# A rotary rotation without a permutation matmul: VectorE shuffles partner rows out of the projection's bank

## The chip, the cores and the metric

The kernel runs on one core of one Trainium2 chip. The metric is device time in microseconds of one execution, as the median of several. The engines are TensorE (PE, with its weight loads as PEld), VectorE (DVE), ScalarE (ACT), GpSimd (POOL) and the queue that issues most transfers (SP). Each works through its own list of instructions in order and waits on semaphores for the others.

## The reference

Two transformer blocks over 1024 tokens of width 1024, in float32, one after the other. Only the first half of the first block's attention concerns the change: four "differential" heads, each with two q and two k vectors of 64 rows, of which the first 16 rows are rotated by position.

```python
h = rmsnorm(x, norm1_g[l])
proj = jnp.einsum('bsd,de->bse', h, w_in[l])
dq, dk, dv, fq, fk, fv, fg = jnp.split(proj, SPLITS, axis=-1)
dq = rope_partial(dq.reshape(B, S, DIFF_HEADS, 2, DIFF_DH), cos, sin)
dk = rope_partial(dk.reshape(B, S, DIFF_HEADS, 2, DIFF_DH), cos, sin)
...
def rope_partial(t, cos, sin):            # half = 8
    t1 = t[..., :half]
    t2 = t[..., half:ROPE_DIM]
    return jnp.concatenate([t1 * c - t2 * s, t2 * c + t1 * s, t[..., ROPE_DIM:]], axis=-1)
...
p = softmax(mask(q1 k1)) - lam * softmax(mask(q2 k2));  od = rmsnorm(p v, subln_g) * (1 - lam_init)
```

After these come eight "fox" heads with a decay bias and no rotation, the output projection, a gated feed-forward layer, and the second block.

## The kernel before

Everything lies transposed: 128 rows of features on the partitions, 1024 tokens in two halves of 512 columns along the free side. A float32 product is made of three faster ones: each operand is split into a high and a low part, and for every 128-row step PE issues high by high (L1810), low weights by high (L1812) and high weights by low (L1815), each 128x512. I call these three a group; a projection of 128 features for one half is eight groups into one PSUM bank. The weights come from DRAM in pieces of four steps; ACT rounds a piece to its high part (L2421) and POOL subtracts for the low part (L2670, "lows"). PE has to have both.

The first block's attention runs in units: a0 to a3 (differential, one head each), then b0 to b3 (fox). While unit n goes through scores, softmax and values, the dense groups of unit n+1's q, k and v projection are put between its steps as filler; a0's own projection runs at the start, beside the first norm. For each half of q and of k of units a0 to a3 the steps are:

- DVE evacuates the bank into a stage buffer and multiplies by the norm factor `rstd` (for q also by 0.125): L2080, L2082.
- Three groups later PE multiplies the stage by a permutation matrix in plain float32, which brings each row its partner row eight rows away (L1868), into the next dense bank.
- DVE multiplies that bank by the table of sines into a second stage buffer (L2089), POOL multiplies the first stage by cosines (L2676) and adds both (L2694).
- ACT copies the sum to its high part (L2504, L2505), POOL makes the low parts in two instructions (L2707, L2709), SP moves some of them to other partitions, and the scores may start.

A sub-norm closes each differential unit: ACT squares (L2546), PE sums over partitions (L1936), DVE turns the sum into a mean (L2165), ACT takes Ln and Exp (L2552, L2556, each behind a table load), POOL does five instructions per half (L2716 to L2725).

Buffers: five stage buffers (four more in the start), handed out in turn; whoever takes one waits for the events that gave it back. In units a0 to a3 the dense groups use PSUM banks 6 and 7 in turn, the value products bank 5, transposes bank 4, scores banks 0 to 3.

The order of each engine's list is not written by hand. `work_order` records steps; `engine_orders` then places them on the engines by a table of estimated durations and the waits among them, and each engine's program is written out in that order. So a change of one step can move others on all engines.

Of the kernel before, what the change touches and what calls it, by code (L numbers as in the profile page):

```python
# [7 lines left out]
F = mybir.dt.float32  # L8
# [136 lines left out]
class Tiles:  # L145


    def __init__(self, nc, ctx, args, out):
# [26 lines left out]
        self.ones = self.new("ones", [128, 128], F, 512)  # L175
        self.perm = self.new("perm", [128, 128], F, 512)
        self.maskb = self.new("maskb", [128, 128], BF, 256)
# [112 lines left out]
class Order:  # L290
# [520 lines left out]
class Attention:  # L811
# [51 lines left out]
    def group_steps(self, g, u, a, c, jobs, slot, last):  # L863
# [40 lines left out]
        if u.kind == DIFF:  # L904
            yield
            squares, roots = [], []
            for half in range(2):
                i, gi = O.next_stage()
                O.step("sub_square", g=g, half=half, i=i, gi=gi, out=out)
                squares.append(i)  # L910
            means = [O.next_stage() for _ in range(2)]
            for half in range(2):
                i = squares[half]
# [7 lines left out]
                if half:  # L921
                    O.step("sub_roots", g=g, roots=roots)
                O.bank_given[b] = [("sub_mean", (g, half))]
# [3 lines left out]
                yield  # L927
        if self.direct is None:
# [128 lines left out]
def work_order(T):  # L1057
    O = Order(T)
# [85 lines left out]
    def first_tiles(evac_q, evac_k):  # L1144
        gen = O.dense_together([("w_fg", 0, fg_evac), ("w_in", 0, evac_q), ("w_in", 4, evac_k)], 0, ready, first=first_ready_in)
        for k in range(7):
            next(gen)
            yield
        O.rstd_ready = O.rsqrt([("mix", [[("acc", 7)]] * 2)], S, EPS1, "rstd", banks=[6, 7])
        yield from gen  # L1150
        O.step("fg_log")
# [626 lines left out]


def spans(n):  # L1780

# [11 lines left out]
def tensor_program(e, w, sg, T, steps):  # L1793
    PS = T.PS
    for s in steps:
# [55 lines left out]
        elif kind == "row_sum":  # L1851
# [10 lines left out]
            m.then_inc(*sg.up("rs_sum", (s["n"], half)))  # L1862
        elif kind == "rotate":
            for event in s["given"]:
                w.wait_ge(*sg.at(*event))
            w.wait_ge(*sg.at("evac", s["key"]))
            w.wait_ge(*sg.at("perm", 0))
            e.matmul(PS[:, s["b"], :], T.perm[:, :], T.stage[s["i"]], start=True, stop=True).then_inc(*sg.up("permuted", s["key"]))  # L1868
        elif kind == "by_tokens":
# [77 lines left out]
def vector_program(e, w, sg, T, steps):  # L1947
    PS = T.PS
    stage, sm, rstd = T.stage, T.sm, T.rstd
    for s in steps:  # L1950
# [122 lines left out]
        elif kind == "qkv_evac":  # L2073
# [9 lines left out]
            m.then_inc(*sg.up("evac", s["key"]))  # L2083
        elif kind == "rotate":
            for event in s["gj"]:
                w.wait_ge(*sg.at(*event))
            w.wait_ge(*sg.at("table", 0))
            w.wait_ge(*sg.at("permuted", s["key"]))
            e.tensor_tensor(stage[s["j"]], PS[:, s["b"], :], T.TABF[:, 1, cols(s["half"])], ALU.mult).then_inc(*sg.up("rot_sin", s["key"]))  # L2089
        elif kind == "by_tokens":  # L2090
# [569 lines left out]
def gpsimd_program(e, w, sg, T, steps):  # L2660
    stage = T.stage
    for s in steps:
        kind = s["kind"]
        if kind == "split" and s["piece"].n >= BY_VECTOR:
# [3 lines left out]
            for reader in piece.read_by:  # L2668
                w.wait_ge(*sg.at("w_sum", reader.n))
            e.tensor_tensor(T.wl[piece.v][:, 0:m], T.wv[piece.v][:, 0:m], T.wh[:, piece.h, 0:m].bitcast(F), ALU.subtract).then_inc(  # L2670
                *sg.up("w_lo", piece.n))
        elif kind == "rotate":
            key, st = s["key"], stage[s["i"]]
            w.wait_ge(*sg.at("table", 0))
            w.wait_ge(*sg.at("permuted", key))
            e.tensor_tensor(st, st, T.TABF[:, 0, cols(s["half"])], ALU.mult).then_inc(*sg.up("rot_cos", key))  # L2676
        elif kind == "operand_lo" and s["by"] == "gpsimd":
# [12 lines left out]
        elif kind == "rotate_add":  # L2690
            key, st = s["key"], stage[s["i"]]
            w.wait_ge(*sg.at("rot_cos", key))
            w.wait_ge(*sg.at("rot_sin", key))
# [51 lines left out]
def sync_program(e, w, sg, T, steps):  # L2745
    args, cst, stage = T.args, T.args["cst"], T.stage
    for s in steps:
# [3 lines left out]
        elif kind == "consts":  # L2751
            e.dma_start(T.ident[:, :], cst[:, C_ID:C_ID + 128]).then_inc(*sg.up("ident", 0, by=16))
            e.dma_start(T.perm[:, :], cst[:, C_PERM:C_PERM + 128]).then_inc(*sg.up("perm", 0, by=16))
        elif kind == "x_load":
# [360 lines left out]
```

## Time and profile before

| | before |
|---|---|
| timed runs, us | 2413.95, 2414.42, 2415.20 (median 2414.42) |
| profiled execution, first to last instruction, us | 2411.1 |
| PE busy | 2375.6 us, 99% |
| DVE busy | 1871.7 us, 78% |
| ACT busy | 1090.3 us, 45% |
| POOL busy | 1115.1 us, 46% |
| granted TensorE clock, mean | 0.997 |

The profiled execution has no time of its own besides its span; the median of the timed runs is 3.3 us above that span, which is what lies before the first and after the last instruction and between runs. Shares of busy time are averages over stages with different limits. A matmul's record is longer than the distance to the next one, since matmuls overlap: what one costs is read from the starts around it.

### The profile page before, as it was taken

What the parts mean: (1) busy time and instruction counts of PE and PEld (TensorE: products, weight loads), DVE (VectorE), ACT (ScalarE), POOL (GpSimd) and SP (SyncE); (2) the same over time, 40 slices, a digit from 0 to 9 for tenths busy, and PEclk for the clock granted to TensorE, in tenths of its full rate; (3) what the DMA queues carried; (4) which work ended last, traced back from release to release, by engine and by line L of the source; (5) the groups of instructions that cost most, each with busy time, mean ns of one, the idle gap of its engine ahead of it and who ended that gap; (6) DMA issues with size and microseconds to landing.
All of it is one profiled execution on the core that took longest, in us unless ns stands there. A gap on an engine that the chain in (4) does not pass through costs nothing.

```text
span 2411.1 us, 31839 instructions
## 1 busy us (share of the span) xinstructions
PE 2375.6 (99%) x11414; PEld 1951.6 (81%) x11414; DVE 1871.7 (78%) x2405; ACT 1090.3 (45%) x1868; POOL 1115.1 (46%) x786
## 2 busy tenths in 40 slices
PE   9999999999999999999999999999999999999998
PEld 7777788878878888888887888887878888888887
DVE  6777757674587898889967956778288898999986
ACT  6455555553453333344435436555263333544433
POOL 4666651211534665454453462431253466555553
PEclk9999999999999999999999999999999999999998
DMA  5311321132122232354522872223223444754532
GB/s 162 83 47 54 89 66 36 56 116 76 55 70 79 88 114 93 120 194 132 179 60 93 186 174 58 62 59 109 82 66 127 145 149 157 238 169 148 170 98 105
DMA packets 228171, 263.06 MB, mean 109 GB/s; under 512 B 18224, under 2 KB 139824, under 8 KB 227888
## 3 DMA queue, kind: packets, MB, share of 16 engines
q1 hardware_dynamic: 224416, 248.72, 32.9%
q0 software_dynamic: 3168, 11.54, 2.6%
q8 instruction: 92, 1.51, 0.3%
q10 hardware_dynamic: 432, 0.79, 0.1%
q14 instruction: 63, 0.52, 0.1%
HBM read 169.74 MB, written 60.82 MB: 96 GB/s over the span
## 4 chain that ended last, share of the span: by engine, by line
PE 88%; DVE 4%; POOL 3%; ACT 2%; issue 1%; DMA 1%; SPq 0%; POOLq 0%; ACTq 0%; DVEq 0%
PE PS L1810 25%; PE PS L1815 25%; PE PS L1812 25%; PE PS L1908 3%; PE PS L1895 2%; PE PS L1929 2%; PE PS L1926 2%; PE PS L1889 2%; PE PS L1892 1%; POOL stage L2694 0%; DVE X L2300 0%; PE PS L1894 0%; DMA stage<-scr_mix 0%; POOL stage_r L2707 0%; POOL stage_r L2709 0%
## 5 line engine op out<-in xcount | busy, mean ns | idle before, releaser
L1810 PE MATMUL PS<-R,wh 128*128 128x512 f32 x2872 | 1135.8, 395 | 4.8 <-DVE X L2300 1.4
L1815 PE MATMUL PS<-R,wh 128*128 128x512 f32 x2872 | 1122.1, 391 | 2.7 <-DVE R L2248 2.0
L2670 POOL TENSOR_TENSOR lows<-values,wh 128x512 fp32r<-128x512 f32 (+1 forms) x486 | 684.8, 1414 | 905.2 <-ACT wh L2421 743.6
L1812 PE MATMUL PS<-R,lows 128*128 128x512 f32 x2564 | 1001.2, 390 | 1.0 <-POOL lows L2670 1.0
L1815 PEld LDWEIGHTS PS<-R,wh 128*128 128x128 f32 x2872 | 539.5, 188 | 120.7 <-DVE R L2248 3.8
L1810 PEld LDWEIGHTS PS<-R,wh 128*128 128x128 f32 x2872 | 540.7, 188 | 114.0 <-issue 3.9
L2421 ACT ACTIVATE wh<-values 128x512 fp32r<-128x512 f32 (+2 forms) x487 | 302.1, 620 | 620.4 <-PE PS L1815 614.7
L1812 PEld LDWEIGHTS PS<-R,lows 128*128 128x128 f32 x2564 | 482.4, 188 | 94.8 <-issue 3.6
L2300 DVE TENSOR_TENSOR X<-PS,X 128x1024 f32<-128x1024 f32 x154 | 187.3, 1217 | 23.5 <-PE PS L1815 22.9
L2670 POOL TENSOR_TENSOR late_r<-late,wh 128x512 fp32r<-128x512 f32 x77 | 108.0, 1402 | 123.7 <-DVE values L2197 54.9
L2537 ACT ACTIVATE PT<-PS 128x512 fp32r<-128x512 f32 (+1 forms) x200 | 108.4, 553 | 100.2 <-PE PS L1908 86.9
L1812 PE MATMUL PS<-R,late_r 128*128 128x512 f32 x308 | 120.0, 389 | 0.0
L1895 PE MATMUL PS<-R 128*128 128x512 f32 (+2 forms) x288 | 115.7, 402 | 0.0
L2100 DVE TENSOR_REDUCE sm<-PS 128x1 f32<-128x128 f32 (+7 forms) x128 | 95.4, 751 | 24.3 <-PE PS L1895 23.4
L1908 PE MATMUL PS<-ident,Pb 128*128 128x128 f32 x720 | 106.9, 274 | 5.4 <-DVE Pb L2112 2.5
L1889 PE MATMUL PS<-R 128*128 128x512 f32 (+2 forms) x288 | 106.2, 369 | 5.7 <-ACT P L2520 3.8
L2124 DVE TENSOR_TENSOR_SCAN Pb<-TABF,vec 128x128 f32<-128x128 f32 (+3 forms) x64 | 95.9, 1503 | 18.1 <-PE PS L1908 10.4
L1908 PEld LDWEIGHTS PS<-ident,Pb 128*128 128x128 f32 x720 | 85.4, 141 | 25.4 <-issue 9.7
L2289 DVE TENSOR_TENSOR R1f<-R1f 128x512 f32<-128x512 f32 x88 | 95.7, 1116 | 12.9 <-ACT R1f L2625 11.9
L2203 DVE TENSOR_TENSOR stage<-PS,stage 128x512 f32<-128x512 f32 x143 | 96.2, 681 | 8.4 <-PE PS L1815 6.7
L2520 ACT ACTIVATE Pb<-PS,sm 128x128 f32<-128x128 f32 (+3 forms) x96 | 70.9, 739 | 58.6 <-DVE sm L2100 57.4
L2147 DVE TENSOR_TENSOR PT<-PS,PT 128x512 fp32r<-128x512 f32 (+1 forms) x120 | 74.8, 632 | 27.6 <-ACT PT L2537 26.9
(279 smaller groups left out, 3036.8 us busy)
## 6 DMA issues: line engine op xcount, KB each, us to landing
scr_hid<-R1f SPq DMA_DIRECT2D x160, 256.0 KB, 2.8
values<-w_in_dram SPq DMA_DIRECT2D x88, 256.0 KB, 2.9
R1f<-scr_hid SPq DMA_DIRECT2D x88, 256.0 KB, 3.7
R0f<-scr_hid SPq DMA_DIRECT2D x86, 256.0 KB, 3.8
values<-w_ff_dram SPq DMA_DIRECT2D x60, 256.0 KB, 3.0
values<-w_ff_dram SPq DMA_DIRECT2D x100, 128.0 KB, 2.4
R<-R SPq DMA_DIRECT2D x96, 128.0 KB, 2.3
X<-X POOLq DMA_DIRECT2D x22, 512.0 KB, 5.9
```

The source lines that it names most:

```text
L1810: e.matmul(PS[:, b, :], wh, high, start=s["start"], stop=False, skip_group_check=on)
L1812: e.matmul(PS[:, b, :], wl, high, start=False, stop=False, skip_group_check=on)
L1815: m = e.matmul(PS[:, b, :], wh, low, start=False, stop=s["stop"], skip_group_check=on)
L1889: e.matmul(S2[:, k0:k1], q, u.KH[:, a, k0:k1], start=True, stop=False)
L1895: m = e.matmul(S2[:, k0:k1], q, u.KL[:, a, k0:k1], start=False, stop=True)
L1908: m = e.transpose(PS[:, s["tb"], at:at + 128], T.Pb[:, s["slot"], par, 128 * kt:128 * kt + 128], T.ident[:, :])
L2124: e.tensor_tensor_scan(dst[:, ::-1], bt[:, ::-1], T.zeros(n), 1.0, ALU.mult, ALU.add).then_inc(*sg.up("p", j["key"]))
L2203: e.tensor_tensor(stage[s["i"]], PS[:, s["b"], :], stage[s["k"]], ALU.add).then_inc(*sg.up("seven", s["key"]))
L2300: e.tensor_tensor(x, T.PS[:, s["b"]:s["b"] + 2, :], x, ALU.add).then_inc(*sg.up("block", s["key"]))
L2421: e.activation(T.wh[:, piece.h, 0:m], T.wv[piece.v][:, 0:m], ACT.Copy).then_inc(*sg.up("w_hi", piece.n))
L2537: e.activation(T.PT[:, s["x"], 0, 0:m], PS[:, s["tb"], 0:m], ACT.Copy, bias=bias).then_inc(*sg.up("pt_hi", key))
L2670: e.tensor_tensor(T.wl[piece.v][:, 0:m], T.wv[piece.v][:, 0:m], T.wh[:, piece.h, 0:m].bitcast(F), ALU.subtract).then_inc(*sg.up("w_lo", pi ...
```

## The change

The permutation matmul, its matrix and its bank go. When q's or k's projection is complete in its bank, DVE reads it twice: a shuffle within each 32 partitions writes the partner rows into one stage buffer, and a product with a table of cosines, already multiplied by the norm factor, writes the other (for q also times 0.125). POOL multiplies the partner rows by sines times norm factor (for q, first by 0.125) and adds. Both tables are multiplied by the norm factor once, in place: the cosines by DVE, the sines by POOL (`table_rstd`). The evacuation now takes both stage buffers together, and the split into high and low parts is recorded at once, not three groups later. The sub-norm's two sums go to two banks (5 and 4), one behind the other, and its means come after both.

```diff
@@ project @@
-            def rotate(half, i, which=which, split=split):
-                b, given = self.side_bank()
-                j, gj = self.next_stage()
+            def rotate(half, i, j, which=which, split=split):
                 key = (u.name, which, half)
-                self.step("rotate", key=key, half=half, i=i, j=j, gj=gj, b=b, given=given)
+                self.step("rotate", key=key, half=half, j=j)
                 self.step("rotate_add", key=key, i=i, j=j)
-                self.bank_given[b] = [("rot_sin", key)]
                 self.stage_given[j] = [("rot", key)]
                 u.rotated = ("rot", key)
                 split(half, i)
...
             def evac(half, b, t, after=after, which=which):
                 i, gi = self.next_stage()
                 key = (u.name, which, half)
+                if u.kind == DIFF and which < 2:
+                    j, gj = self.next_stage()
+                    self.step("turn_evac", key=key, t=t, half=half, b=b, i=i, gi=gi + gj, j=j)
+                    self.bank_given[b] = [("evac", key)]
+                    after(half, i, j)
+                    return
...
@@ group_steps, sub-norm @@
-                b = self.OB
-                O.step("sub_sum", g=g, half=half, i=i, b=b, given=O.claim(b))
-                yield
-                j, gj = means[half]
+                b, given = O.next_t() if half else (self.OB, O.claim(self.OB))
+                O.step("sub_sum", g=g, half=half, i=squares[half], b=b, given=given)
+                O.bank_given[b] = [("sub_mean", (g, half))]
+                sums.append(b)
+            yield
+            for half, (i, b) in enumerate(zip(squares, sums)):
+                j, gj = O.next_stage()
                 O.step("sub_norm", g=g, half=half, i=i, j=j, gj=gj, b=b)
                 roots.append((half, i, j))
...
@@ tensor_program @@
-        elif kind == "rotate":
...
-            e.matmul(PS[:, s["b"], :], T.perm[:, :], T.stage[s["i"]], start=True, stop=True).then_inc(*sg.up("permuted", s["key"]))
@@ vector_program @@
-            e.tensor_tensor(stage[s["j"]], PS[:, s["b"], :], T.TABF[:, 1, cols(s["half"])], ALU.mult).then_inc(*sg.up("rot_sin", s["key"]))
+            e.tensor_tensor(T.TABF[:, 0, :], T.TABF[:, 0, :], rstd[:, :], ALU.mult).then_inc(*sg.up("cosines", 0))
+        elif kind == "turn_evac":
+            ps, cosines = PS[:, s["b"], :], T.TABF[:, 0, cols(s["half"])]
...
+            e.stream_shuffle(stage[s["j"]], ps, PARTNERS)
+            if s["key"][1] == 0:
+                m = e.scalar_tensor_tensor(stage[s["i"]], ps, 0.125, cosines, ALU.mult, ALU.mult)
+            else:
+                m = e.tensor_tensor(stage[s["i"]], ps, cosines, ALU.mult)
@@ gpsimd_program @@
+            e.tensor_tensor(T.TABF[:, 1, :], T.TABF[:, 1, :], T.rstd[:, :], ALU.mult).then_inc(*sg.up("sines", 0))
         elif kind == "rotate":
-            key, st = s["key"], stage[s["i"]]
...
-            e.tensor_tensor(st, st, T.TABF[:, 0, cols(s["half"])], ALU.mult).then_inc(*sg.up("rot_cos", key))
+            key, partner, sines = s["key"], stage[s["j"]], T.TABF[:, 1, cols(s["half"])]
...
+            if key[1] == 0:
+                e.tensor_scalar(partner, partner, 0.125, None, ALU.mult).then_inc(*sg.up("rot_part", key))
+                w.wait_ge(*sg.at("rot_part", key))
+            e.tensor_tensor(partner, partner, sines, ALU.mult).then_inc(*sg.up("rot_sin", key))
```

Since the planner places all steps anew, instructions move on every engine. Three places show it. A line number of the new kernel is higher than that of the same line before (L2670 is now L2684, L2694 is L2715, L2707 is L2728, L2165 is L2179, L1810 is L1819).

The first is POOL's list in the start, from the rotation's first instruction on. Before ("early" and "stage" are stage buffers, "R" the units' operands):

```order
L2676 TENSOR_TENSOR stage<-stage,TABF 128x512
L2694 TENSOR_TENSOR stage<-stage,early 128x512
L2676 TENSOR_TENSOR stage<-stage,TABF 128x512
L2707 TENSOR_TENSOR stage_r<-stage,R_50 64x512
L2709 TENSOR_TENSOR stage_r<-stage,R_50 64x512
L2694 TENSOR_TENSOR stage<-stage,early 128x512
L2676 TENSOR_TENSOR stage<-stage,TABF 128x512 x2
```

And after, from the product of the sine table on:

```order
L2690 TENSOR_TENSOR TABF<-TABF,rstd 128x1024
L2684 TENSOR_TENSOR lows<-values,wh 128x512
L2696 TENSOR_SCALAR stage<-stage 128x512
L2698 TENSOR_TENSOR stage<-stage,TABF 128x512
L2696 TENSOR_SCALAR stage<-stage 128x512
L2698 TENSOR_TENSOR stage<-stage,TABF 128x512
L2715 TENSOR_TENSOR stage<-stage 128x512 x2
L2698 TENSOR_TENSOR early<-early,TABF 128x512
```

Both halves of q now go through scaling and sine product before the first sum. Behind these rows, before the next weight split, the new list has six low parts, two sums and a sine product more, with two low parts behind that split; the list before had six low parts and two sums more, and no scaling.

The second place is DVE's list at the end of unit a0, around the two means of the sub-norm (L2165, now L2179). Before, from the first mean to the next (the reduction is a score row's maximum, `Pb` its softmax):

```order
L2165 TENSOR_SCALAR stage<-PS 128x512
L2106 RECIPROCAL sm<-sm 128x1
L2114 TENSOR_SCALAR Pb<-Pb,sm 128x384
L2147 TENSOR_TENSOR PT<-PS,PT 128x384
L2100 TENSOR_REDUCE sm<-PS 128x1
L2165 TENSOR_SCALAR stage<-PS 128x512
```

After, the same stretch:

```order
L2179 TENSOR_SCALAR stage<-PS 128x512
L2114 TENSOR_REDUCE sm<-PS 128x1
L2120 RECIPROCAL sm<-sm 128x1
L2128 TENSOR_SCALAR Pb<-Pb,sm 128x512
L2114 TENSOR_REDUCE sm<-PS 128x1
L2120 RECIPROCAL sm<-sm 128x1
L2124 TENSOR_SCALAR sm<-sm 128x1
L2126 SCALAR_TENSOR_TENSOR Pb<-P_62,sm,Pb 128x512
L2114 TENSOR_REDUCE sm<-PS 128x1
L2179 TENSOR_SCALAR stage<-PS 128x512
```

The second mean moved behind the softmax of two jobs of 512 columns, which stood behind it before.

The third place is PE's list at the same point, from a unit's second sum on. Before (L1868 is the permutation):

```order
L1936 MATMUL PS<-stage,ones 128x512
L1868 MATMUL PS<-stage,perm 128x512
L1810 MATMUL PS<-R_49,wh 128x512
L1812 MATMUL PS<-R_49,lows 128x512
L1815 MATMUL PS<-R_49,wh 128x512
L1926 MATMUL PS<-PT,R_50 128x256 x2
L1926 MATMUL PS<-PT,R_50 128x128 x2
```

After:

```order
L1939 MATMUL PS<-stage,ones 128x512 x2
L1819 MATMUL PS<-R_49,wh 128x512
L1821 MATMUL PS<-R_49,lows 128x512
L1824 MATMUL PS<-R_49,wh 128x512
L1819 MATMUL PS<-R_49,wh 128x512
L1821 MATMUL PS<-R_49,lows 128x512
L1824 MATMUL PS<-R_49,wh 128x512
L1892 MATMUL PS<-R_50 128x512
```

Both sums stand together, the permutation is gone, and the scores of the first 512-column job follow after two dense groups.

## Rows read from the trace of the kernel before

**Rows 1.** Chain that ended last, share of the span by engine.
```profile
PE 88%; DVE 4%; POOL 3%; ACT 2%; issue 1%; DMA 1%; SPq 0%; POOLq 0%; ACTq 0%; DVEq 0%
```

**Rows 2.** Line 1868, the permutation: duration min/median/max ns, first and last start us.
```profile
L1868 PE MATMUL PS<-stage,perm x32: 590/592/596, 46.0 to 235.6; 128*128 128x512 f32 x32
```

**Rows 3.** Timeline of PE around a permutation: start us, us, line, operation, count.
```profile
45.80 0.40 PE L1815 MATMUL PS<-R,wh 128*128 128x512 f32 x1
46.04 1.02 PE L1868 MATMUL PS<-stage,perm 128*128 128x512 f32 x2
...
47.13 0.40 PE L1812 MATMUL PS<-R,lows 128*128 128x512 f32 x1
47.37 0.39 PE L1815 MATMUL PS<-R,wh 128*128 128x512 f32 x1
```

**Rows 4.** Stretches: us, busy us of PE, PEld, DVE, ACT, POOL; clock, DMA, GB/s.
```profile
77.00:131.00 54.00, 52.02 (x293) 40.83 (x292) 46.98 (x93) 28.97 (x66) 25.61 (x20) 1.00 0.19 49
...
131.10:196.80 65.70, 61.40 (x320) 47.55 (x320) 48.54 (x84) 34.06 (x66) 43.85 (x32) 1.00 0.21 57
196.80:263.70 66.90, 63.13 (x328) 48.76 (x327) 48.08 (x84) 34.81 (x67) 43.69 (x32) 1.00 0.25 72
263.70:330.00 66.30, 65.58 (x350) 52.99 (x350) 44.75 (x82) 36.33 (x70) 36.63 (x27) 1.00 0.22 62
```

**Rows 5.** PE's waits, first 360 us: total us, times, longest.
```profile
PE PS L1889 <- ACT P L2520: 3.8, 4, 1.2
```

**Rows 6.** DVE by form: busy us, mean ns, idle before; last row min/median/max ns.
```profile
L2089 DVE TENSOR_TENSOR stage<-PS,TABF 128x512 f32<-128x512 f32 x13 | 8.9, 682 | 5.8 <-DMA R<-stage_r 2.9 <-PE PS L1868 2.8
...
L2152 DVE COPY mix<-PS 128x256 f32<-128x256 f32 x16 | 6.6, 415 | 2.6 <-PE PS L1929 2.6
...
L2067 DVE TENSOR_TENSOR_SCAN Pb<-Pb 128x1024 f32<-128x1024 f32 x1 | 3.1, 3059 | 2.6 <-ACT Pb L2497 2.6
...
L2062 DVE TENSOR_SCALAR Pb<-Pb,vec 128x1024 f32<-128x1024 f32 x1 | 0.7, 743 | 0.0
...
L1993 DVE TENSOR_TENSOR mix<-mix,SQ x7: 1212/1881/2041, 10.8 to 30.5; 128x1024 f32<-128x1024 f32 x7
```

**Rows 7.** POOL by form, first 360 us: busy us, mean ns, idle before.
```profile
L2676 POOL TENSOR_TENSOR stage<-stage,TABF 128x512 f32<-128x512 f32 x16 | 21.4, 1347 | 34.3 <-PE PS L1868 33.8
L2694 POOL TENSOR_TENSOR stage<-stage 128x512 f32<-128x512 f32 x13 | 18.2, 1404 | 4.1 <-DVE stage L2089 4.0
...
L2721 POOL TENSOR_SCALAR stage<-stage,sm 128x512 f32<-128x512 f32 x8 | 5.8, 724 | 0.8
```

**Rows 8.** Timeline of the start: DVE's first evacuations, the weight split, PE's wait.
```profile
42.58 1.29 DVE L2059 TENSOR_TENSOR Pb<-PS,rstd 128x512 f32<-128x512 f32 x2 [2.85 <-PE PS L1815]
...
71.33 2.51 POOL L2670 TENSOR_TENSOR lows<-values,wh 128x512 fp32r<-128x512 f32 x2
...
72.65 0.50 PE L1812 MATMUL PS<-R,lows 128*128 128x512 f32 x1 [1.01 <-POOL lows L2670]
```

**Rows 9.** Timeline of the first seam, units a0 to a1, all engines.
```profile
131.10 1.02 PE L1936 MATMUL PS<-stage,ones 128*128 128x512 f32 x2
...
135.21 0.69 DVE L2165 TENSOR_SCALAR stage<-PS 128x512 f32<-128x512 f32 x1 [0.84 <-PE PS L1936]
...
144.11 0.50 PE L1889 MATMUL PS<-R 128*128 128x512 f32 x1 [1.22 <-ACT P L2520]
144.54 1.87 DVE L2112 SCALAR_TENSOR_TENSOR Pb<-P,sm,Pb 128x512 f32<-128x512 f32 x1
144.58 1.28 POOL L2725 TENSOR_TENSOR mix<-mix,stage 128x512 f32<-128x512 f32 x1
...
146.55 0.63 PE L1908 MATMUL PS<-ident,Pb 128*128 128x128 f32 x4 [0.53 <-DVE Pb L2112]
147.79 0.50 PE L1810 MATMUL PS<-R,wh 128*128 128x512 f32 x1 [0.61 <-DVE stage L2089]
...
151.25 1.75 POOL L2725 TENSOR_TENSOR mix<-mix,stage 128x512 f32<-128x512 f32 x1
```

More of the change, by code:

```diff
@@ L175, in __init__ @@
         self.ones = self.new("ones", [128, 128], F, 512)
-        self.perm = self.new("perm", [128, 128], F, 512)
         self.maskb = self.new("maskb", [128, 128], BF, 256)
@@ L910, in group_steps @@
                 squares.append(i)
-            means = [O.next_stage() for _ in range(2)]
+            sums = []
             for half in range(2):
-                i = squares[half]
                 yield
-                b = self.OB
-                O.step("sub_sum", g=g, half=half, i=i, b=b, given=O.claim(b))
-                yield
-                j, gj = means[half]
+                b, given = O.next_t() if half else (self.OB, O.claim(self.OB))
[5 more added lines that the diff above has]
+                j, gj = O.next_stage()
                 O.step("sub_norm", g=g, half=half, i=i, j=j, gj=gj, b=b)
                 roots.append((half, i, j))
-                if half:
-                    O.step("sub_roots", g=g, roots=roots)
-                O.bank_given[b] = [("sub_mean", (g, half))]
+            O.step("sub_roots", g=g, roots=roots)
+            for half, i, j in roots:
                 out = ("sub", (g, half))
@@ L926, in group_steps @@
                 O.stage_given[j] = [out]
-                yield
+            yield
+            yield
+            yield
         if self.direct is None:
@@ L1149, in first_tiles @@
         O.rstd_ready = O.rsqrt([("mix", [[("acc", 7)]] * 2)], S, EPS1, "rstd", banks=[6, 7])
+        O.step("table_rstd", rstd=list(O.rstd_ready))
         yield from gen
@@ L1774, in work_order @@
     return O.steps
+PARTNERS = [*range(8, 16), *range(8), *range(16, 32)]
 def spans(n):
@@ L1862, in tensor_program @@
             m.then_inc(*sg.up("rs_sum", (s["n"], half)))
-        elif kind == "rotate":
[L1864 to L1867, printed above, removed]
-            e.matmul(PS[:, s["b"], :], T.perm[:, :], T.stage[s["i"]], start=True, stop=True).then_inc(*sg.up("permuted", s["key"]))
         elif kind == "by_tokens":
@@ L2083, in vector_program @@
             m.then_inc(*sg.up("evac", s["key"]))
-        elif kind == "rotate":
-            for event in s["gj"]:
+        elif kind == "table_rstd":
+            w.wait_ge(*sg.at("table", 0))
+            for event in s["rstd"]:
                 w.wait_ge(*sg.at(*event))
-            w.wait_ge(*sg.at("table", 0))
-            w.wait_ge(*sg.at("permuted", s["key"]))
-            e.tensor_tensor(stage[s["j"]], PS[:, s["b"], :], T.TABF[:, 1, cols(s["half"])], ALU.mult).then_inc(*sg.up("rot_sin", s["key"]))
+            e.tensor_tensor(T.TABF[:, 0, :], T.TABF[:, 0, :], rstd[:, :], ALU.mult).then_inc(*sg.up("cosines", 0))
+        elif kind == "turn_evac":
+            ps, cosines = PS[:, s["b"], :], T.TABF[:, 0, cols(s["half"])]
+            for event in s["gi"]:
+                w.wait_ge(*sg.at(*event))
+            w.wait_ge(*sg.at("cosines", 0))
+            w.wait_ge(*sg.at("dense", (s["t"], s["half"])))
+            e.stream_shuffle(stage[s["j"]], ps, PARTNERS)
[3 more added lines that the diff above has]
+                m = e.tensor_tensor(stage[s["i"]], ps, cosines, ALU.mult)
+            m.then_inc(*sg.up("evac", s["key"]))
         elif kind == "by_tokens":
@@ L2671, in gpsimd_program @@
                 *sg.up("w_lo", piece.n))
-        elif kind == "rotate":
-            key, st = s["key"], stage[s["i"]]
-            w.wait_ge(*sg.at("table", 0))
-            w.wait_ge(*sg.at("permuted", key))
-            e.tensor_tensor(st, st, T.TABF[:, 0, cols(s["half"])], ALU.mult).then_inc(*sg.up("rot_cos", key))
+        elif kind == "table_rstd":
+            w.wait_ge(*sg.at("table", 0))
+            for event in s["rstd"]:
+                w.wait_ge(*sg.at(*event))
+            e.tensor_tensor(T.TABF[:, 1, :], T.TABF[:, 1, :], T.rstd[:, :], ALU.mult).then_inc(*sg.up("sines", 0))
+        elif kind == "rotate":
+            key, partner, sines = s["key"], stage[s["j"]], T.TABF[:, 1, cols(s["half"])]
+            w.wait_ge(*sg.at("sines", 0))
+            w.wait_ge(*sg.at("evac", key))
+            if key[1] == 0:
+                e.tensor_scalar(partner, partner, 0.125, None, ALU.mult).then_inc(*sg.up("rot_part", key))
+                w.wait_ge(*sg.at("rot_part", key))
+            e.tensor_tensor(partner, partner, sines, ALU.mult).then_inc(*sg.up("rot_sin", key))
         elif kind == "operand_lo" and s["by"] == "gpsimd":
@@ L2691, in gpsimd_program @@
             key, st = s["key"], stage[s["i"]]
-            w.wait_ge(*sg.at("rot_cos", key))
             w.wait_ge(*sg.at("rot_sin", key))
```

1 line of the change is left out of this document (removed).

## The prediction

> **What bounds the kernel now.** I read the page first. PE is busy for 99% of the span (the table above), and 88% of the chain that ended last is PE's [rows 1], so what leaves PE's queue can come off the end, unless something else then makes PE wait. Next the line that goes: the permutation matmul, 32 records for 16 rotations, all between 46 and 236 us [rows 2]. Then the timeline around one of them, for what it really costs, since matmul records overlap [rows 3]. Then the stretches in which rotations run, against the one without [rows 4], PE's list of waits [rows 5], and the two places where the new steps lie on a chain that PE waits for: the start [rows 7, 8] and the seam between two attention units [rows 9].
>
> The reader is to see that PE is bound, but not by its work alone. In the two stretches with rotations it is idle for 4.3 of 65.7 us and 3.8 of 66.9; in the stretch after them, the same attention without rotations beside it, for 0.7 of 66.3 [rows 4]. DVE is the next engine: 72 to 74% in those stretches, 87% in the first unit (47.0 of 54.0 us). POOL stands at 65 to 67% [rows 4]. The waits are short: most come from the softmax chain [rows 5], one from POOL's weight split [rows 8], one from a bank that the rotation holds [rows 9].
>
> **The matmul.** The L1815 in front of the first permutation starts at 45.80, the second matmul behind it at 47.13; ordinary matmuls of 512 columns start 0.23 us apart (47.13 to 47.37), which would have made 46.26 [rows 3]. So one permutation costs PE 0.87 us, and 16 cost 13.9 us. That is the most the change takes out of PE's queue. Six of them stand before the first scores, two in the first unit, eight in the next two units.
>
> **VectorE.** Before: an evacuation and a product with sines, both reading PSUM. After: a shuffle and a product with cosines, both reading PSUM. The products cost the same 0.68 us [rows 6]. No shuffle is in the trace. It lies between the PSUM copy of half the columns (0.41 us) and half of the 1024-column scan (1.53 us) [rows 6]; I take 0.68, the nearest row of the same size that reads PSUM. Then DVE's sum is unchanged, with one more instruction, the product of the cosine table with the norm factor: 1024 columns from two SBUF inputs, 1.2 to 2.0 us by such a row [rows 6]. At 1.53 us per shuffle DVE would carry 13.6 us more. The Trainium skill ("VectorE: DVE Perf Modes", section "The perf-mode tier table") says that a shuffle only has a one-element-per-cycle form and gives about 2400 ns for 2048 elements; an estimate from that is 0.6 to 0.75 us for 512, and the sum would stay as it is. No run so far shows it.
>
> **GpSimd.** Before: cosine product and sum, 1.35 and 1.40 us [rows 7]. After: sine product and sum, the same sizes, and for the eight q halves a scaling by 0.125, which I price like the kernel's other tensor-scalar of this shape, 0.72 us [rows 7]: 5.8 us. The table product (1024 columns) is twice a 512-column product, about 2.6 us.
>
> **The start.** The weight split that PE waits for at 72.65 (1.0 us idle) is POOL's instruction of 71.33, which stands behind the rotation's work [rows 8]; the order keeps it there. After the change POOL has ahead of it four sine products, four sums, six low parts and two scalings: 14 of about 1.36 and 2 of 0.72 us, 20.5 us [rows 7]. They can begin once DVE has q's first half: fg evacuations end at 43.87 (42.58 and 1.29) [rows 8], table 1.2 to 2.0, one tensor-scalar of 0.74 [rows 6], shuffle and product 1.3, so at 47.2 to 47.9. The split then ends at about 47.9 + 20.5 + 1.3 = 69.7. PE, five permutations ahead, wants it at 71.6 - 4.35 = 67.3: a wait of 2.4 instead of 1.0. Behind it stand two low parts and the next split, so that one ends at 73.7, while the first piece feeds PE for four groups of three matmuls, 2.8 us, to 72.5: another 1.2. Price: 2.6 us of the 5.2. The split order also puts the first scores four groups later; the low parts of k's second half end at about 72.4 and their transfers later, so a few tenths more: I take 3.0. What is left is 2.2 us. The two permutations of the first unit give 1.7, in a unit where DVE is 87% busy.
>
> A rule of the Trainium skill speaks against the start. The row shows DVE's product of this shape between 1.2 and 2.0 us while POOL splits weights beside it [rows 6]: up to 0.8 us of delay. "SBUF — State Buffer" (section "SBUF: two separate sides") says that a VectorE instruction with two SBUF inputs and a GpSimd one that reads SBUF exclude each other for the whole instruction. Here both engines multiply their tables at the same moment, so by the rule DVE would stand until POOL's product ends, at about 45.1, and end at 46.3, 0.4 later than I assume; the gain would be 6.5 instead of 6.9.
>
> **The seam.** At a unit's end a sub-norm runs: sums on PE, means on DVE, Ln and Exp on ACT, five POOL instructions per half. Before, the second mean comes at 135.21, 4.1 us after the first sum, and POOL's halves end at 145.9 and 153.0 [rows 9]. After, the second mean stands behind the softmax of two 512-column jobs (the order below), work that ended at 146.4 before (144.54 and 1.87); counted from the first sum I put it at 11 us, so POOL's first half ends at about 21 us after the sum, not 14.8. ACT's table loads and both functions shift with it and stand in front of the next job's exponent. And the next unit's q evacuation now takes two stage buffers at once; the second q half gets one of its two from POOL's first half, and k's second half needs that bank. So dense work restarts at about 21 + 1.4 = 22.5 us after the sum. In between PE has 13 groups of 0.69 us (9.0), and eight score jobs, transposes, products and sums that I put at 8.6 from their columns: 17.6. It waits 5. Before, dense work restarted 16.7 us after the sum, with three waits of 1.22, 0.53 and 0.61 [rows 9], about 3.0 with the pipe's refill; the last of these was the bank held by the rotation, and goes. So each of the two seams with rotations behind them gives back about 2 of its unit's 3.5 us, and leaves 1.5.
>
> The stretch behind 263 us and all later stages issue the same work, with other stage buffers here and there; I count nothing. One load of 64 KB less in SP's first 20 us: nothing waits there.
>
> **Sum.** 2.2 + 1.7 + 1.5 + 1.5 = 6.9 us. The profiled execution spans 2411.1 us; the timed runs have their median 3.3 us above that span, which I leave as it is. 2411.1 - 6.9 + 3.3 = 2407.5.
>
> **Rivals.**
> 1. *The whole matmul time comes off.* The planner hides the longer chains; waits neither grow nor shrink. For it: the stretch without rotations loses only 0.7 us [rows 4], and the bank wait goes. Against: POOL's row of work at the start is a plain count. 2414.4 - 13.9 = 2400.5.
> 2. *Swallowed.* Softmax sets the pace: in the first unit DVE has only 7.0 of 54.0 us free, at the seams the delayed Exp holds back all 3.5 us, and shuffles may cost more than a product. What stays is the start's 2.2: 2412.2. Against: the units with 73% busy DVE.
> 3. *Slower.* DVE works in order. If the shuffle of q's second half gets its last buffer not from POOL's first half but from the second, 7.1 us later (145.9 to 153.0), it holds every max and normalisation behind it, and PE runs out of scores: 7.1 us at each of two seams, 14.2 on top, 2421.7. It decides once the new waits exceed 13.9 us in all. For it: five stage buffers serve six demands at a seam. Against: in the built order that evacuation waits for the first half's buffers, and only k's first half for the second.
>
> **Chances.** My forecast (half of the matmul time given back as waits, own range 2404 to 2411) 0.50, the whole time off 0.22, swallowed 0.20, slower 0.08. 0.2% is 4.8 us, about what a measurement of this kernel tells from no change. Faster by more: the whole of rival 1, eight tenths of my case (to 2409.6 of its range) and a tenth of rival 2, 0.64; within: 0.28; slower: 0.08. For eight in ten the range reaches from rival 1 to just past rival 2: 2400 to 2413.5.
>
> **What would show it.** The steps: no permutation line; shuffles of 0.6 to 0.75 us; POOL's scalings at 0.7. At the start PE idle for 2 to 3 us before a matmul with low weights, released by POOL. At the seams waits of about 5 us together behind the sums, released by ACT's exponents or DVE's evacuation, and ACT's Ln and Exp some 6 us later after the sum than before. Stretches of the two middle units near 64 us instead of 66. Wrong if the middle stretches shrink by 3.5 or more (waits hidden, rival 1), if they stay (rival 2), or if PE waits behind a shuffle that waits for POOL's second half (rival 3).

## The result, and the profile after

The changed kernel is slower: 2421.43 us (median of 8 runs), the kernel before 2414.18 in the same session, ratio 1.0032 with a 95% interval of 1.0023 to 1.0042. That is 7.2 us the other way, outside the range I gave. The profiled execution spans 2419.2 us, before 2411.1.

Where it is lost is read from the start of each group's first matmul (L1810 before, L1819 after; there are 2872). Time after minus time before, by the number of the group:

| group | 60 | 80 | 120 | 160 | 200 | 240 | 400 | 2871 |
|---|---|---|---|---|---|---|---|---|
| before, us | 55.3 | 71.3 | 132.2 | 188.3 | 244.9 | 293.6 | 520.4 | 2395.2 |
| after, later by us | -2.5 | 4.2 | 7.3 | 9.2 | 9.9 | 9.8 | 7.9 | 8.2 |

Everything happens in the first 330 us. By stage, from the first scores to the first sum of each unit's sub-norm (in brackets the groups issued in it):

| | first scores at | unit a0 | a1 | a2 | a3 |
|---|---|---|---|---|---|
| before | 76.84 (85) | 54.3 (35) | 65.7 (47) | 66.9 (48) | 59.8 (49) |
| after | 82.25 (89) | 59.9 (34) | 62.4 (44) | 67.4 (48) | 60.1 (49) |

The groups are filler, so they have to be counted too: one takes PE 0.69 us (three matmuls 0.23 us apart). Counted so, the start lost 2.7 us (5.4 later, with four groups more done), the first unit 6.3 (one group less), a1 won 1.2 (3.3 shorter, but with three groups less), a2 and a3 lost 0.4 each. From here on "net" means counted like this.

The same stretches in the view by windows of the changed kernel (columns as in [rows 4]):

```profile
40.00:82.25 42.25, 35.96 (x161) 29.28 (x159) 20.54 (x30) 18.60 (x25) 36.16 (x25) 0.92 0.30 82
82.25:142.10 59.85, 53.03 (x290) 41.43 (x289) 50.59 (x99) 29.41 (x69) 31.80 (x24) 0.97 0.17 45
142.10:204.53 62.43, 56.94 (x300) 45.59 (x299) 43.11 (x79) 32.35 (x62) 43.81 (x33) 0.97 0.21 59
204.53:271.88 67.35, 60.82 (x317) 48.39 (x316) 44.07 (x86) 34.14 (x65) 46.48 (x34) 0.97 0.27 71
```

And the first of them before:

```profile
40.00:76.84 36.84, 35.83 (x160) 27.40 (x158) 17.58 (x23) 18.81 (x25) 28.18 (x22) 1.00 0.35 94
```

PE is idle for 6.3, 6.8, 5.5 and 6.5 us, before for 1.0, 2.0, 4.3 and 3.8 (the last three from [rows 4]), and its granted clock, 1.00 in every row before, is 0.92 to 0.97. So the matmuls went out of PE's queue, and PE got waits and a slower clock in their place. PE's largest waits of the first 360 us, from its list (to be held against [rows 5] and the 1.0 us of [rows 8]):

```profile
PE PS L1929 <- ACT PT L2551: 6.6, 4, 2.6
PE PS L1892 <- ACT Pb L2534: 6.0, 5, 1.7
PE PS L1879 <- DVE stage L2085: 5.9, 1, 5.9
```

**The start.** The one wait of 5.9 us, in rows picked from the timeline of all engines:

```profile
42.85 2.40 POOL L2690 TENSOR_TENSOR TABF<-TABF,rstd 128x1024 f32<-128x1024 f32 x1 [4.31 <-ACT rstd L2503]
...
44.02 2.32 DVE L2091 TENSOR_TENSOR TABF<-TABF,rstd 128x1024 f32<-128x1024 f32 x1
...
46.26 1.77 DVE L2065 TENSOR_SCALAR Pb<-Pb,vec 128x1024 f32<-128x1024 f32 x1
...
49.44 1.50 POOL L2696 TENSOR_SCALAR stage<-stage 128x512 f32<-128x512 f32 x1 [1.96 <-DVE stage L2100]
...
53.48 2.28 DVE L2070 TENSOR_TENSOR_SCAN Pb<-Pb 128x1024 f32<-128x1024 f32 x1
...
53.87 2.98 POOL L2698 TENSOR_TENSOR stage<-stage,TABF 128x512 f32<-128x512 f32 x1
...
61.89 1.26 POOL L2730 TENSOR_TENSOR stage_r<-stage,R 64x512 fp32r<-64x512 f32 x1
...
66.37 0.69 DVE L2085 TENSOR_TENSOR stage<-PS,rstd 128x512 f32<-128x512 f32 x1 [2.14 <-DMA R<-stage_r]
...
67.21 1.09 PE L1879 MATMUL PS<-ident,stage 128*128 128x128 f32 x4 [5.94 <-DVE stage L2085]
...
68.52 0.63 PE L1821 MATMUL PS<-R,lows 128*128 128x512 f32 x1
...
68.95 0.63 PE L1824 MATMUL PS<-R,wh 128*128 128x512 f32 x1
...
72.27 0.39 PE L1821 MATMUL PS<-R,lows 128*128 128x512 f32 x1
...
72.50 0.39 PE L1824 MATMUL PS<-R,wh 128*128 128x512 f32 x1
...
73.17 1.29 POOL L2684 TENSOR_TENSOR lows<-values,wh 128x512 fp32r<-128x512 f32 x1
...
76.23 1.29 POOL L2730 TENSOR_TENSOR R<-early,R 64x512 fp32r<-64x512 f32 x1
...
82.25 0.28 PE L1892 MATMUL PS<-R 128*128 128x256 f32 x1
```

The last low parts of q's first half and of k before:

```profile
54.69 1.27 POOL L2709 TENSOR_TENSOR stage_r<-stage,R 64x512 fp32r<-64x512 f32 x1
...
69.97 1.28 POOL L2709 TENSOR_TENSOR R<-stage,R 64x512 fp32r<-64x512 f32 x1
```

Read it upward from 67.21. PE stands at the transposes of v's second half. They wait for its evacuation (66.37), the tenth user of the nine stage buffers of the start. It gets the buffer of q's first half, which comes back when the low part has been carried off by DMA, and GpSimd ends that low part at 63.15 (in the kernel before the same part ended at 55.96). The built order names the wait:

```
L2085 TENSOR_TENSOR stage<-PS,rstd 128x512 [waits s_ql10,s_dense,s_ql00,s_qk_hi]
```

After 5.9 us of idling PE's matmuls of 512 columns start 0.43 us apart instead of 0.23, until 72: the granted clock is 0.50 there, the lower of its two levels, 1.2 instead of 2.4 GHz. A second thing is late in the same rows: GpSimd ends k's last low part, which the first scores need, at 77.52, before at 71.25.

**The second seam.** DVE's two means of a1's sub-norm, what follows on ACT, and PE:

```profile
206.00 0.68 DVE L2179 TENSOR_SCALAR stage<-PS 128x512 f32<-128x512 f32 x1
...
220.60 0.68 DVE L2179 TENSOR_SCALAR stage<-PS 128x512 f32<-128x512 f32 x1
221.31 0.63 ACT L2566 ACTIVATE stage<-stage 128x512 f32<-128x512 f32 x1 [3.22 <-DVE stage L2179]
221.96 1.28 ACT L2570 ACT_TABLE_LOAD   x1
...
224.31 0.47 ACT L2551 ACTIVATE PT<-PS 128x384 fp32r<-128x384 f32 x1
...
224.83 0.67 PE L1929 MATMUL PS<-PT,R 128*128 128x256 f32 x4 [2.61 <-ACT PT L2551]
```

Both sums are on PE at 204.5 and 206.6, but the second mean comes 14.6 us after the first. Its wait in the order is the same as above, for the buffer of the next unit's q (`s_ql10`, `s_ql00`). ACT works in order, so Ln, table load and Exp stand ahead of the copy of transposed weights that PE needs.

### The profile page after: what moved, and what is told of

Same layout as the page of the kernel before. It is cut to its first block, busy times and chain, and to the rows that moved or that the text cites. A ratio compares the mean times of both kernels' runs of the same rounds, so it can differ in the third digit from the quotient of the medians.

```text
span 2419.2 us, 31775 instructions
## 1 busy us (share of the span) xinstructions
PE 2369.4 (98%) x11382; PEld 1950.1 (81%) x11382; DVE 1870.2 (77%) x2422; ACT 1086.8 (45%) x1868; POOL 1137.0 (47%) x795
## 4 chain that ended last, share of the span: by engine, by line
PE 87%; DVE 5%; POOL 3%; ACT 2%; issue 2%; DMA 1%; SPq 0%; POOLq 0%; DVEq 0%; ACTq 0%
PE PS L1819 25%; PE PS L1824 25%; PE PS L1821 25%; PE PS L1911 3%; PE PS L1898 2%; PE PS L1932 2%; PE PS L1929 2%; PE PS L1892 2%; PE PS L1895 1%; DVE R L2266 1%; DVE X L2314 0%; POOL stage L2698 0%; PE PS L1897 0%; POOL lows L2684 0%; DVE X L2197 0%
## 5 line engine op out<-in xcount | busy, mean ns | idle before, releaser
L1819 PE MATMUL PS<-R,wh 128*128 128x512 f32 x2872 | 1134.1, 395 | 4.9 <-DVE X L2314 1.4
L2684 POOL TENSOR_TENSOR lows<-values,wh 128x512 fp32r<-128x512 f32 (+1 forms) x486 | 691.0, 1427 | 893.1 <-ACT wh L2435 732.3
L1819 PEld LDWEIGHTS PS<-R,wh 128*128 128x128 f32 x2872 | 541.5, 189 | 113.6 <-DVE X L2314 3.7
L2684 POOL TENSOR_TENSOR late_r<-late,wh 128x512 fp32r<-128x512 f32 x77 | 107.8, 1400 | 121.0 <-DVE values L2211 54.8
L1929 PE MATMUL PS<-PT,R 128*128 128x256 f32 x480 | 91.1, 285 | 9.8 <-ACT PT L2551 6.6
```

Source lines behind the costliest of these rows:

```text
L1819: e.matmul(PS[:, b, :], wh, high, start=s["start"], stop=False, skip_group_check=on)
L1929: e.matmul(o, lhs, T.PT[:, x, 0, kk], start=s["first"] and n == 0, stop=False)
```

## The experiments

Each is timed in five rounds against the kernel before; "at group 400" is the difference to the kernel before in the profiled executions where the units are over (the changed kernel: +7.9). Behind that point most variants move by less than 2 us up to group 1680 (e10 by 4.6), and then some shift by up to 5.6 us in the second attention's start, where no edit acts and the planner's order moves as well. So the column is the better measure of an edit where it acts, and a few us between two medians can come from behind it. But it is one execution per kernel, whose time lies up to 2.2 us from the median of its kernel (e9), so differences of 2 us in it are not shown to be real.

| | median, us | before, us | ratio, 95% | at group 400 | first scores | a0 | a1 | a2 |
|---|---|---|---|---|---|---|---|---|
| e1 | 2420.64 | 2413.90 | 1.0018 to 1.0036 | +6.2 | 82.1 | 59.8 | 60.8 | 67.6 |
| e2 | 2417.74 | 2413.90 | 1.0004 to 1.0022 | +4.2 | 81.2 | 59.3 | 60.2 | 67.5 |
| e3 | 2422.75 | 2413.90 | 1.0023 to 1.0048 | +8.9 | 82.5 | 60.8 | 61.6 | 67.6 |
| e4 | 2411.76 | 2413.90 | 0.9981 to 0.9999 | -2.0 | 77.1 | 54.2 | 63.8 | 66.7 |
| e5 | 2416.62 | 2414.14 | 1.0004 to 1.0021 | +3.3 | 81.4 | 56.5 | 61.6 | 67.4 |
| e6 | 2412.59 | 2414.14 | 0.9987 to 1.0005 | -1.9 | 82.1 | 57.2 | 60.5 | 62.4 |
| e7 | 2421.22 | 2414.14 | 1.0017 to 1.0039 | +3.6 | 79.0 | 56.3 | 65.5 | 66.5 |
| e8 | 2414.36 | 2414.14 | 0.9993 to 1.0011 | -0.5 | 80.0 | 53.5 | 62.6 | 67.6 |
| e9 | 2411.99 | 2414.88 | 0.9975 to 0.9992 | -0.1 | 81.4 | 56.4 | 62.0 | 64.4 |
| e10 | 2415.48 | 2414.88 | 0.9999 to 1.0017 | -2.7 | 78.1 | 55.3 | 62.2 | 65.2 |
| e11 | 2411.99 | 2414.88 | 0.9981 to 0.9998 | -1.5 | 76.9 | 58.0 | 63.2 | 65.2 |
| e12 | 2415.56 | 2413.84 | 0.9997 to 1.0015 | +0.5 | 77.8 | 56.1 | 62.9 | 67.4 |
| e13 | 2411.87 | 2413.84 | 0.9989 to 1.0006 | -3.9 | 77.7 | 57.2 | 61.4 | 64.6 |
| e14 | 2413.04 | 2413.84 | 0.9988 to 1.0005 | -5.0 | 77.9 | 57.4 | 61.5 | 63.0 |

**e1: the scaling as one instruction of two operations.**

```
-e.tensor_scalar(partner, partner, 0.125, None, ALU.mult)
+e.tensor_scalar(partner, partner, 0.125, 1.0, ALU.mult, ALU.mult)
```

> Same order on every engine as the changed kernel; only GpSimd's scaling of q's partner rows is written with two operations (times 0.125, times 1.0) instead of one. In the changed kernel that instruction took 1.49 us, eight times, where the sub-norm's two-operation one took 0.82. Theory A (GpSimd's chain ahead of PE's transposes is too long): if the two-operation form takes 0.8 us, the buffer PE waits for at 61 to 67 us comes free 1.3 us earlier, and the time falls by 1.5 to 4 us, to 2417 to 2420. Theory B (the new sub-norm order makes the loss, at the ends of the units): no change within 1 us. If the form itself has no effect (still 1.49 us), the time stays at 2421.

GpSimd's line L2696 in the changed kernel, then in e1 (duration min/median/max in ns):

```profile
L2696 POOL TENSOR_SCALAR stage<-stage x8: 1486/1490/1500, 49.4 to 237.5; 128x512 f32<-128x512 f32 x8
```

```profile
L2696 POOL TENSOR_SCALAR stage<-stage x8: 617/620/628, 49.2 to 235.7; 128x512 f32<-128x512 f32 x8
```

The instruction fell from 1.49 to 0.62 us, seven of 12 us on GpSimd went, and the time moved by 0.8 us, less than expected. In the start PE still waits 5.6 us. GpSimd's two sums now meet DVE's scan, and its low part another VectorE instruction with two inputs in SBUF:

```profile
53.17 4.53 POOL L2715 TENSOR_TENSOR stage<-stage 128x512 f32<-128x512 f32 x2
53.30 3.32 DVE L2070 TENSOR_TENSOR_SCAN Pb<-Pb 128x1024 f32<-128x1024 f32 x1
...
60.22 1.27 DVE L2074 SCALAR_TENSOR_TENSOR PT<-Pb,vec,PT 32x1024 fp32r<-32x1024 f32 x1 [1.72 <-ACT PT L2499]
60.28 2.34 POOL L2730 TENSOR_TENSOR stage_r<-stage,R 64x512 fp32r<-64x512 f32 x1
```

Two sums take 2.5 us elsewhere, the low part 1.26. The scan had cost GpSimd 1.7 us in the changed kernel already (the product of 2.98 us), so of the 1.7 us that two scalings save, the scan takes back 0.3 and the other instruction 1.1: q's low part ends at 62.62 instead of 63.15.

**e2: no scaling at all**, the factor in the constant tables.

```
-            if key[1] == 0:
-                e.tensor_scalar(partner, partner, 0.125, None, ALU.mult).then_inc(*sg.up("rot_part", key))
...
+    c[:, C_COS:C_COS + 2 * S] *= np.float32(8 ** -0.5)
```

> The factor 0.125 goes into the constant tables (each times the root of one eighth, for q and k alike), so GpSimd's eight scalings go. Theory A: two scalings of 1.49 us fewer ahead of the buffer that PE waits for, so the 5.9 us wait shrinks to about 3, and 1.5 us less in front of other sums; 2413 to 2418. If the clock then stays up at the start, another 2.4 us. Theory B (sub-norm): 2420 to 2422.

In the range of theory A: the wait before the transposes is 1.9 us instead of 5.9, the clock stays at 1.00 up to 77 us, and 3.7 us come off. But the first scores come only 1.1 us earlier, six groups have gone ahead of them, and a0 is as long as it was: PE idles there instead, and 77 to 131 us has a clock of 0.87.

**e3: one stage buffer more in the start** (the tenth for ten users).

```
-    O.lend_stages(EARLY, [])
+    O.lend_stages(EARLY + [9], [])
...
+    att1.p2_given += spare
```

> One stage buffer more during the start (ten for the ten that the first unit's projection takes). Theory A: the evacuation of v's second half no longer waits for the first q buffer to come back, so the 5.9 us wait and the half clock behind it (2.4 us) go, and a wait of 3 to 4 us for GpSimd's weight split comes instead: 2414 to 2418. Theory B: the start's wait is no loss of its own, since other work moves up behind it; no change within 1.5 us.

A miss for theory A. The wait is gone, and nothing is won: PE ran seven groups ahead, and then waited for k's low parts, which GpSimd ends at 79.2 us here, and without filler for the softmax. Two rows of PE's timeline and the stretch of the first unit:

```profile
82.53 0.55 PE L1894 MATMUL PS<-R 128*128 128x256 f32 x1 [2.98 <-DMA R<-R]
...
89.40 0.69 PE L1894 MATMUL PS<-R 128*128 128x384 f32 x1 [3.20 <-ACT Pb L2536]
```

```profile
77.00:131.00 54.00, 44.30 (x205) 34.60 (x204) 42.44 (x78) 25.12 (x56) 34.50 (x26) 0.78 0.24 61
```

I read this as two chains in parallel: the buffer is one, GpSimd's row of work up to k's low parts the other. e10 lifts both.

**e4: the kernel before with only the new sub-norm sums.**

```
+                b, given = O.next_t() if half else (self.OB, O.claim(self.OB))
...
```

> The kernel before, with only the sub-norm's two sums put into two banks and the means taken behind both. Theory A (the start and GpSimd's chain make the loss): 2413 to 2417, at most one wait of PE behind Ln and Exp. Theory B (the new sub-norm order makes it): 2420 or more, since the 13.9 us of the permutations stay.

2.1 us faster, below both ranges. Theory B (the new order of the sub-norm makes the loss) is out for the sub-norm alone. It also means that the rotation has to be held against e4, not against the kernel before: at group 400 it costs 9.9 us (+7.9 against -2.0).

**e5: in the first unit, k's sine product and sum on VectorE.**

```
@@ vector_program @@
+        elif kind == "rotate" and s["key"][:2] == ("a0", 1):
...
+            e.tensor_tensor(partner, partner, sines, ALU.mult).then_inc(*sg.up("evac", ("sine", *key)))
```

> The changed kernel, but in the first unit (a0) VectorE does the sine product and the sum of k's two halves; GpSimd keeps the rest. Theory C (the serial row of GpSimd's rotation work from 49 to 77.5 us sets when the first scores start, 82.25 us where the kernel before had 76.84, and PE's filler runs out meanwhile): four instructions of 1.3 us fewer in that row, first scores at about 77 us, and the time 4 to 6 us less, 2415 to 2418. Theory E (five stage buffers, two of which each half of q and k now holds from its evacuation on, keep the dense banks occupied in the units, so PE has no filler beside the softmax): first scores earlier, but unit a0 still takes 59 to 60 us; total down 2 at most if the gain is given back, as it was with one buffer more.

4.8 us faster, as theory C had it for the time, but not by its road: k's low parts are done at 73.5 instead of 77.5 us, while the first scores moved by 0.8. Now the other chain holds them. VectorE's new products stand beside GpSimd's sums, q's low part ends at 64.5 us, and PE waits for v's buffer longer than before the edit:

```profile
68.49 1.08 PE L1883 MATMUL PS<-ident,stage 128*128 128x128 f32 x4 [6.58 <-DVE stage L2089]
```

**e6: a sixth stage buffer in the differential units**, taken from the seven weight buffers.

```
+            if self.reserve:
+                self.lend_stages([19 + piece.v], [("dense", event)])
...
```

> The changed kernel with a sixth stage buffer from the first unit to the end of the differential units, taken from the seven weight buffers. Theory E: unit a0 (first scores to first sum, 59.9 us, before 54.3) shrinks to 55 to 57, and the waits behind the transposes of 2.1 and 2.6 us shrink; 2413 to 2418. Theory C: start and first unit as they are; 2420 to 2422.5. If one weight buffer less costs by itself, it shows as waits for weights (high or low parts), and the time may rise.

8.8 us faster than the changed kernel, a little more than theory E had it, but mostly not where theory E had it. The first unit wins 1.3 us net; a1 wins 4.0 (1.9 shorter, with three groups more) and a2 5.0 (67.4 to 62.4 us). The net loss of 8 us up to the end of the first unit stays. The second mean at the second seam comes 1.7 us after the first, and PE has no wait there between 199 and 214 us:

```profile
201.27 0.68 DVE L2188 TENSOR_SCALAR stage<-PS 128x512 f32<-128x512 f32 x1
202.94 0.69 DVE L2188 TENSOR_SCALAR stage<-PS 128x512 f32<-128x512 f32 x1 [0.99 <-PE PS L1948]
```

**e7: the kernel before, each permutation issued twice.**

> The kernel before, with each of its 16 permutation matmuls issued twice. It prices the removed matmul where it stood. If PE's queue is the bound throughout (rival 1 of the prediction), 13.9 us more: 2428. If the units have slack in PE beside the softmax (rival 2), only the six in the start cost, 5.2 us: 2419; my forecast had half hidden: 2421 to 2424.

7.1 us more in the median, where I had half of the time hidden. In the profiled execution 3.6 us of 8.5 come up to group 400; the rest lies behind the last permutation and says nothing of its price, so that the median fits is luck. By group 80 the six of the start have cost 5.1 us, 0.85 each. The units a1 and a2, with eight of them, are as long as before (65.5 and 66.5). The matmul cost its full price only where PE had no other slack: in the start. (PE's order moved in this run too, so the price by stage is approximate.)

**e8 to e11: the edits together, and a control.** e8 is e2 with e5; e9 adds e6, e10 adds e3 to that; e11 is e4 with the sixth buffer.

> Both: no scaling on GpSimd, and k's rotation of the first unit on VectorE. Theory C: 8.2 us less in GpSimd's row before the first scores, so they start at 75 to 76 us; the start is then as in the kernel before or better, and the time 2409 to 2413. Theory E: unit a0 still 59 us or more, and 2414 to 2417.

> The three edits together: no scaling on GpSimd, k's rotation of the first unit on VectorE, a sixth stage buffer in the units. If the chain of GpSimd in the start and the buffers in the units are two separate losses, they add: 2414.4 - 8.8 = 2405 to 2408. If both are one (the first unit's lack of filler), 2410 to 2414.

> As e9, with the tenth stage buffer in the start. With one buffer more alone the wait at 61 to 67 us came back as a wait for GpSimd's low parts. Now that GpSimd's row before the first scores is 8 us shorter, the wait of 6.4 us and the half clock behind it should go for good: 4 to 8 us less than e9, 2398 to 2404. If the first scores still start at 80 us, or PE's filler is used up before them, no gain over e9, as with one buffer more alone.

> The kernel before with the new sub-norm sums and the sixth stage buffer, permutations kept: the control for e6. If the sixth buffer only pays for what the new rotation takes (a second buffer from the evacuation on), it brings nothing here: 2410 to 2413, as with the new sums alone (2411.8). If a sixth buffer is worth 9 us to any version, 2403 to 2406.

e8 undoes the loss (-0.5 at group 400) with a0 at 53.5 us; its first scores come at 80.0, not at the 75 to 76 that I expected, and its time lies 1.4 us above theory C's range. The sixth buffer adds nothing to it in these stretches (e9), a miss: net, it won 2.7 us in a1 and 2.5 in a2, and lost 1.4 before the first scores and 5.0 in a0. e9 is 2.9 us faster than the kernel before in the median, the fastest by its ratio. In e10 the first scores come at 78.1, against 81.4 in e9, which lacks only the buffer, and 82.5 in e3, which has it alone, so the two chains of the start do hide each other. The time is a plain miss, 2415.5 where I had 2398 to 2404; 3.6 us are given back between groups 400 and 1400. e11, the control, came out as expected: without the new rotation the sixth buffer brings nothing (-1.5 against -2.0).

**e12 to e14: the old rotation in the first unit alone**, then with the sixth buffer, then with e1's form too.

```
+            after = by_tokens if which == 2 else turn_first if u.name == "a0" else rotate if ...
```

> The changed kernel with the first unit's (a0) rotation as in the kernel before (evacuation, permutation matmul, sines on VectorE, cosines on GpSimd), and the tables multiplied by the norm factor behind it; units a1 to a3 as in the changed kernel. If the loss lies in the start and first unit alone: first scores at 76.5 to 78 us, first sum at 131 to 134, unit a1 still 3 us shorter than before, and the time 2409 to 2413. If the units a1 to a3 lose too: 2415 to 2419.

> As e12, with the sixth stage buffer in the units. If start and buffers are the two losses: start as before, units a1 and a2 shorter by 3 and 5 us, 2403 to 2408. If e9's lack of a sum holds here too, 2410 to 2413.

> As e13, with the scaling of q's partner rows on GpSimd as one instruction of two operations (0.62 us instead of 1.49, in units a1 to a3 six times): 5 us less on GpSimd, beside other work: 0 to 2 us less than e13.

e12 takes 5.9 us off the median and 7.4 of the 7.9 us at group 400, and PE's idle time and clock in the first unit are again what they were:

```profile
77.00:131.00 54.00, 52.57 (x294) 41.23 (x293) 47.08 (x95) 27.59 (x64) 35.88 (x26) 1.00 0.20 53
```

So most of the loss sits in the first unit's rotation. Units a1 to a3 take 2.0 us less than in the kernel before, with three groups less: net nothing, where e4 wins 1.9 with the permutations. So the new rotation costs those units what the new sums win there, some 2.5 us at group 400 (+0.5 against e4's -2.0). The median is 2.6 us above the range for a loss in the first unit alone, and inside the one for a loss in all units; 4.6 us of the profiled execution come from behind group 400. With the sixth buffer e13 and e14 stand at -3.9 and -5.0 us at group 400. In the profiled executions e13 gives back 1.5 of that, e14 all of it and 2.3 more, and neither median differs from the kernel before clear of noise.

## Why the prediction was wrong

The sum had a gain of 2.2 us for the start, 1.7 for the first unit and 3.0 for the seams. Net, the runs show a loss of 2.7, a loss of 6.3 and a gain of 0.8.

- **The matmul's price**, 0.87 us, was right for the start (0.85 in e7). That it counts in the units was wrong as far as e7 shows it: there it was nearly free, since PE had slack beside the softmax.
- **VectorE**: the shuffle took 0.74 us, where I had 0.68 and bounds of 0.41 to 1.53. The estimate from the figure of the Trainium skill ("VectorE: DVE Perf Modes", section "The perf-mode tier table") was 0.6 to 0.75, and the trace agrees.
- **GpSimd's scaling** was mis-sized: 1.49 us, not 0.72; 11.9 us instead of 5.8. I took the price from a row with another form, two operations, which e1 shows to be the cheap one.
- **The start is the step that failed.** I asked only when GpSimd's weight split would be late, 3.0 us against 5.2. PE met another wait first: v's evacuation, for a buffer that comes back through GpSimd's low part and a DMA. The buffer's name stood in the built order, and I didn't follow it back. With the half clock behind that wait (the clock was a term that I had put at nothing) group 80 came 4.2 us later instead of 2.2 earlier. The wait that I had priced came to 0.3 us. And GpSimd's row was too short in my sum: the split ended at 74.46, not 69.7, and k's last low part at 77.52, not 72.4, so the first scores were 5.4 us late and not four groups and a few tenths. The row began at 49.4 instead of 47.9 (VectorE's tensor-scalar took 1.77 us, not 0.74), the scalings took 1.5 us more, and two instructions beside VectorE's took 2.98 and 2.12 us instead of 1.3.
- **The first unit** was to gain 1.7 us, and lost 5.6 with a group less. Three score jobs run one behind the other from 94.5 to 98.6 us, with PE waiting for the softmax, and the dense group behind them starts at 99.44, when the evacuation of its bank ends; behind 126 us the clock falls again (0.50 from 128 to 130). In e8, e10 and e12 the unit takes 53.5, 55.3 and 56.1 us. In e12 a1's new rotation still runs beside it, with five groups more, so a0's own rotation makes most of the loss. That it's only the late start carried on isn't shown: e5 has 56.5 us with first scores at 81.4.
- **The seams** gave 2.8 us together (a1 -3.3, a2 +0.4), where I had 3.0. That it fits is luck: a1 issued three groups less (2.1 us), and e4 has 2.2 with the permutations and all groups still there. The stretches came to 62.4 and 67.4 us, not near 64 each.
- **The table product** on VectorE ended at 46.34 us, 1.1 behind GpSimd's (45.25). That is the 46.3 which I worked out from the rule of the Trainium skill ("SBUF — State Buffer", section "SBUF: two separate sides"); the trace agrees, and my own term was 0.4 too early.
- **Rival 3** had the size (2421.7) and the kind of mechanism: a buffer that returns through GpSimd and holds VectorE in order. Its place was wrong: v's evacuation in the start and the second mean at the second seam, not the shuffle of q's second half. So its size, twice 7.1 us at the seams, came out by luck. I gave it 0.08, having looked for it at one place only.

What stays open: why the sixth buffer, worth 9.8 us at group 400 on the changed kernel, adds nothing to e8. The stages show where: net, it wins 2.8 to 7.0 us in a1 and a2 together on three kernels (e9 against e8, e11 against e4, e13 against e12), and each time loses 3.9 to 5.0 us in a0; on the changed kernel a0 had lost that already. Why a0 loses, no run shows. The order of every engine moves with nearly every edit, so these runs don't separate the buffer from the new order.

## What to carry to other kernels

When an edit makes a step hold a buffer earlier, list each wait on a buffer in the built order and follow it back to who gives the buffer back; two chains that end at nearly the same time hide each other, so lifting one shows little (first scores 0.3 us later in e3, 0.8 earlier in e5; with all edits in e10 4.1 earlier). Count the filler that a stage issues before calling it shorter. An idle stretch of the bound engine costs more than its length when the clock falls with it. Take a price from a row of the same form, down to the number of operations, and price a removed instruction where it stands: in a stage with slack it may be worth nothing.

## What the runs showed of the hardware

- On GpSimd a tensor-scalar of 128x512 float32 with one operation took 1.49 us, with two operations 0.62 (e1).
- GpSimd's two-input instructions stretch beside DVE's scan: a product of 1.29 us took 2.98 (changed kernel), two sums of 2.5 us took 4.53 (e1), and the scan itself 2.28 (changed kernel) to 3.37 us (e5).
- Behind a wait of 5.9 us, and behind shorter ones of 1.7, 2.1 and 2.6 us that came with further idling, PE's matmuls ran for some us at half clock in the changed kernel: a granted clock of 0.50 (66 to 72, 128 to 130, 186 to 188 and 226 to 228 us), and 0.43 us from one start to the next instead of 0.23.
